# A hybrid scan, retention and attention step: modulation tiles multiplied in four visits instead of seven

## Chip, cores, metric

One core of a Trainium2 chip runs the whole program. The metric is the device time of one execution in microseconds (us), lower is better.

## The reference

Two streams share the weights of two layers: 128 context tokens and 256 latent tokens, 1024 wide. The reference runs them one after the other; the kernel runs both at once, T = 384 columns. Per layer:

```python
sh1, sc1, g1, sh2, sc2, g2 = _modulation(cond, w_ada, b_ada)   # silu(cond) @ w_ada + b_ada, 1024 x 6144
h = _rmsnorm(x, norm1_w) * (1 + sc1) + sh1
u = h @ w_in                                                    # columns for three groups of heads
y_ssd, ssd_state = _ssd(...)        # state-space scan, 8 heads of 64, two directions
y_ret, ret_state = _retention(...)  # retention with fixed decay, 4 heads of 64, two directions
y_mla, ckv, krope = _mla(...)       # latent attention, 4 heads, keys and values from a rank of 128
x = x + g1 * (concat(y_ssd, y_ret, y_mla) @ w_out)
h2 = _rmsnorm(x, norm2_w) * (1 + sc2) + sh2
x = x + g2 * (swiglu(h2 @ ffn_w1) @ ffn_w2)
```

The change concerns when one part of `_modulation` is multiplied: the 2048 columns of w_ada that give sh2 and sc2. They are needed only after attention.

## The kernel before, in words

The program is written by hand, engine by engine: each engine's instructions stand in one fixed order, and semaphores tie the engines together. The order of the calls in TensorE's block is therefore the order on the engine, and a wait holds up all that is behind it. PE is TensorE, DVE VectorE, ACT ScalarE, POOL GpSimd, and SP the engine that issues nearly all loads.

Activations lie channels on partitions, tokens along the row. Wide products run as three passes over rounded high and low halves (L475 to L477, in `split_mm`); ACT makes the high halves of weights (L1015) and DVE the low halves (L1353). All other products, those of this change too, are plain f32, and each shows in the trace as two records.

*Modulation.* `ada_block(p, k, w)` (L498) multiplies rows of w_ada. With w = 2, as in this stretch, one call handles a pair of tiles of 512 KB: for each of two halves it waits for the landing of its tile in one of four buffers of `adas` (L502), issues four products of 32 output columns by 256, one per group of 32 columns of the array, into bank 4 of PSUM (L504), and tells SP by `ada_used` that the buffer is free. The sums accumulate in bank 4 over all eight pairs, k = 0 to 7, so only the last pair ends them. In the profile one pair is 16 records of L504. SP's `load_ada` (L388 to L393) waits until the tile four places earlier is used up and then issues the load. The first four tiles of the part are loaded long ahead. When the last pair is through, DVE copies the sums (L1363, `ada_rows`), TensorE transposes them (L512, `ada_turn`) and DVE adds the bias (L1371).

*The stretch between scan and attention*, on TensorE, in order: end states of retention (L763), queries 0 and 1 (L802), the last states, **pairs 0 and 1**, retention scores of chunk 0 (L773), the rotation of the keys (L816), queries 2 and 3, **pair 2**, the sum of squares of the gated scan output (L823, waits for ACT's squares and for DVE's keys `kr`, L1728), **pair 3**, the rotation of the queries (L829), `ret_values(0)` (L785), `ret_scores(1)`, **pair 4**, `ret_values(1)` (L785 and L790), `ret_scores(2)`, **pair 5**, `ret_values(2)`, the keys of attention (L845), **pair 6**, the means of the retention output (L849), the values of attention (L858), **pair 7**, the variances (L865), then attention with the first half of the output projection between its heads (L877, seen as L475 to L477).

*Beside it.* DVE multiplies each chunk's scores by the decay matrix (L1704, `ret_probs`), which `ret_values` of the chunk waits for (L779); between these it rotates two heads' queries (L1742 to L1744). It takes the square root's inverse of L823's sums (L1381 to L1385, with ACT's L1027 and L1029 ahead). It copies the retention output to `ry` (L1746) when `ret_values(2)` is through, and L849 waits for that copy (L847). After ACT's squares of the centred output (L1264) come ACT's high halves of the mix (L1056) and, behind `ada_rows` on DVE, their low halves (L1405). The first product of the output projection waits for four of these (L926).

Of the kernel before, what the change touches and what calls it, by code (L numbers as in the profile page):

```python
# [102 lines left out]
def program(nc, x_d, const_d, small_d, win_d, wdt_d, wout_d, wf1_d, wf2_d, wada0_d, wada_d, y_d, sssd_d, sret_d, ckv_d, kr_d):  # L103
    with ExitStack() as ctx:
# [364 lines left out]
        def _(pe):  # L469
# [28 lines left out]
            def ada_block(p, k, w=1):  # L498

                for half in range(w):  # L500
                    b = k * w + half
                    pe.wait_ge(ada_in[b % 4], p * 32 + 16 * (b // 4) - 48)  # L502
                    for j in range(4):
                        last = mm(ps[j * CW:(j + 1) * CW, 4, half * 256:half * 256 + 256], cond[:, k, :],  # L504
                                  adas[:, b % 4, j * 256:(j + 1) * 256], start=(b == 0), stop=(b == w * KD - 1))
                    last.then_inc(ada_used, 1)
# [114 lines left out]
            for L in range(DEPTH):  # L621
# [145 lines left out]
                def ret_scores(c):  # L767

                    if c:
                        pe.wait_ge(rprob_ready, L * 3 + c)  # L770
                    for r in range(HR):
                        rows = slice((r % 2) * 64, (r % 2) * 64 + 64)
                        last = mm(ps[:, 2 + r % 2, (r // 2) * P:(r // 2) * P + P], u[rows, U_RK + r // 2, c * P:c * P + P],  # L773
                                  u[rows, U_RQ + r // 2, c * P:c * P + P], start=True, stop=True)
                    last.then_inc(rscore_ps, 1)

                def ret_values(c):

                    pe.wait_ge(rprob_ready, L * 3 + c + 1)  # L779
                    if c:  # L780
                        pe.wait_ge(qr_ready, L * 8 + 4 * c)
                    for m in range(2):
                        outs = [(2 * m + o, ps[o * 64:o * 64 + 64, m, c * P:c * P + P]) for o in range(2)]
                        for r, out in outs:
                            last = mm(out, kvt[:, c, 256 + r * 64:320 + r * 64], rp[:, r % 2, r // 2, :], start=True,  # L785
                                      stop=(c == 0))
                        if c:

                            for r, out in outs:
                                last = mm(out, enter_r[c - 1][:, r * 64:r * 64 + 64], qr[c - 1][:, r // 2, r % 2, :], start=False, stop=True)  # L790
                    last.then_inc(ry_ps, 1)
# [4 lines left out]
                def query(h):  # L796

                    if h >= 2:
                        pe.wait_ge(q_taken, L * HM + h - 1)
                    for k in range(2):  # L800
                        c0 = C_UQ + k * 384 + h * 96
                        last = mm(ps[0:96, h % 2, 0:T], small[:, c0:c0 + 96], u[:, U_MQ + k, :],  # L802
                                  start=(k == 0), stop=(k == 1))
                    last.then_inc(q_ps, 1)
# [12 lines left out]
                query(2)  # L817
                query(3)
                ada_block(L * 6 + 3, 2, 2)
                pe.wait_ge(gsq_ready, L * 4 + 3)  # L820
                pe.wait_ge(kr_ready, L * 3 + 3)
                for m in range(4):
                    last = mm(ps[:, 7, 0:T], ones, sq_c[:, m, :], start=(m == 0), stop=(m == 3))  # L823
                last.then_inc(ms_ready, 1)
                ada_block(L * 6 + 3, 3, 2)
                pe.wait_ge(ret_state, L * 4 + 4)
                pe.wait_ge(q_taken, L * HM + HM)
                for h in range(HM):
# [4 lines left out]
                ret_values(0)  # L833
                ret_scores(1)
                ada_block(L * 6 + 3, 4, 2)
                ret_values(1)
                ret_scores(2)
                ada_block(L * 6 + 3, 5, 2)
                ret_values(2)

                pe.wait_ge(ck_ready, L * 3 + 3)
# [1 line left out]
                for hp in range(2):  # L843
                    c0 = C_UKV + hp * 128
                    mm(ps[:, 2 + hp, 0:512], small[:, c0:c0 + 128], ck[:, 0:512], start=True, stop=True).then_inc(k_ps, 1)  # L845
                ada_block(L * 6 + 3, 6, 2)
                pe.wait_ge(ry_taken, L + 1)  # L847
                for m in range(2):
                    last = mm(ps[:, m, 0:T], cc(K_BD), ry[:, m, :], start=True, stop=True)  # L849
# [3 lines left out]
                for kt in range(4):  # L853
                    if kt == 1:
                        pe.wait_ge(k_ready, L * HM + 2)
                    if kt >= 2:
                        pe.wait_ge(vm_ready, L * 4 + kt - 1)
                    mm(ps[:, 2 if kt % 2 else 7, 0:256], ck[:, kt * P:kt * P + P], wv, start=True, stop=True)\  # L858
                        .then_inc(vm_ps, 1)
                ada_block(L * 6 + 3, 7, 2)  # L860
                pe.wait_ge(q_ready, L * 2 + 2)
                pe.wait_ge(centred, L + 1)
# [1208 lines left out]
```

## Time and profile before

| | |
|---|---|
| median of 3 runs | 1052.37 us (1051.87 to 1052.9) |
| profiled execution, first to last instruction (span) | 1048.6 us |
| busy: PE, DVE, ACT, POOL | 1026.5, 632.1, 439.6, 106.0 us |
| moved by DMA | 159.56 MB, mean 152 GB/s |
| loads of `adas` by SP | 80 of 512 KB, median 5.7 us from issue to landing |
| L504 in all | 640 records, 39.9 us |

How to read it: the profile gives the profiled execution's own time as its span alone; the median of the runs lies 3.8 us above it, for what is ahead of the first instruction and behind the last. The page's busy time is the union of an engine's instructions. A matmul's start is recorded, its end is modelled, and neighbours overlap in the records; the distance between starts tells how long one holds the engine. The stretch between scan and attention lies at 164 to 192 us in layer 0 and at 669 to 698 us in layer 1. In the views, x16 counts the records of a group, and "[0.38 <-DVE kr L1728]" is idle time of the engine before it and what ended it.

### The profile page before, as it was taken

To read this page: it belongs to the slowest core of one execution; us is meant where nothing else is said; L and a number is where in the kernel's file an instruction comes from. 1 tells how busy PE (TensorE), PEld (TensorE's weight loads), DVE (VectorE), ACT (ScalarE), POOL (GpSimd) and SP (SyncE) were. 2 spreads that over 40 slices of the span, in tenths; PEclk is the share of its full clock that TensorE was granted. 3 is DMA by queue.
4 is the path that set the end of the run, shared out by engine and by line. 5 is a ranking of instruction groups with operands and counts; after the bars stand their busy time and mean duration, and the time that the engine had idled before them with its cause. 6 is when DMAs were issued, how large, how long until landed. Compare 5 with 4: busy or idle time off the path is not lost.

```text
span 1048.6 us, 16439 instructions
## 1 busy us (share of the span) xinstructions
PE 1026.5 (98%) x6552; PEld 938.2 (89%) x6552; DVE 632.1 (60%) x1134; ACT 439.6 (42%) x684; POOL 106.0 (10%) x99
## 2 busy tenths in 40 slices
PE   7899999999999999999999999999999999999995
PEld 4698995789999989999999999668999999999995
DVE  6686868868555543534448787886765555543333
ACT  3256445446333332343334655644543333233231
POOL 0004323003000000000100223400200000000100
PEclk9999999999999999999999999999999999999998
DMA  9843245214333478333364224451243333633331
GB/s 383 330 168 124 82 161 216 115 44 165 129 131 133 168 285 321 118 112 114 135 243 161 91 88 161 161 203 41 81 142 134 125 120 120 258 105 111 126 122 60
DMA packets 30678, 159.56 MB, mean 152 GB/s; under 512 B 3424, under 2 KB 4384, under 8 KB 19872
## 3 DMA queue, kind: packets, MB, share of 16 engines
q1 hardware_dynamic: 28896, 146.75, 38.4%
q10 hardware_dynamic: 1728, 12.06, 2.8%
q8 instruction: 38, 0.62, 0.2%
q14 instruction: 16, 0.13, 0.0%
HBM read 156.27 MB, written 2.52 MB: 151 GB/s over the span
## 4 chain that ended last, share of the span: by engine, by line
PE 93%; DVE 3%; ACT 1%; issue 1%; ACTq 1%; DVEq 0%
PE ps L475 26%; PE ps L477 26%; PE ps L476 26%; PE ps L504 3%; PE ps L920 2%; PE ps L900 1%; PE ps L719 1%; PE ps L746 1%; PE ps L909 1%; PE ps L571 1%; PE ps L823 1%; ACTq L1065 1%; PE ps L802 1%; PE ps L710 0%; DVE wlo L1353 0%
## 5 line engine op out<-in xcount | busy, mean ns | idle before, releaser
L475 PE MATMUL ps<-h_hi,whi 128*128 128x386 f32 (+1 forms) x1120 | 384.9, 344 | 0.2
L477 PE MATMUL ps<-h_hi,wlo 128*128 128x386 f32 (+1 forms) x1120 | 379.7, 339 | 0.0
L476 PE MATMUL ps<-h_lo,whi 128*128 128x386 f32 (+1 forms) x1120 | 378.7, 338 | 0.0
L1353 DVE TENSOR_TENSOR wlo<-stage,whi 128x2048 fp32r<-128x2048 f32 (+1 forms) x106 | 223.3, 2106 | 154.4 <-ACT whi L1015 154.4
L1015 ACT ACTIVATE whi<-stage 128x2048 fp32r<-128x2048 f32 (+1 forms) x106 | 185.9, 1754 | 229.1 <-PE ps L477 210.5
L475 PEld LDWEIGHTS ps<-h_hi,whi 128*128 128x128 f32 x1120 | 211.3, 189 | 9.7 <-issue 7.2
L476 PEld LDWEIGHTS ps<-h_lo,whi 128*128 128x128 f32 x1120 | 211.6, 189 | 0.3
L477 PEld LDWEIGHTS ps<-h_hi,wlo 128*128 128x128 f32 x1120 | 210.6, 188 | 0.0
L475 PE MATMUL ps<-hid_hi,whi 128*128 128x384 f32 x352 | 118.3, 336 | 0.0
L477 PE MATMUL ps<-hid_hi,wlo 128*128 128x384 f32 x352 | 118.3, 336 | 0.0
L476 PE MATMUL ps<-hid_lo,whi 128*128 128x384 f32 x352 | 118.3, 336 | 0.0
L1401 DVE COPY shifted<-ps 128x4 f32<-128x4 f32 x55 | 8.8, 160 | 104.8 <-PE ps L477 104.3
L477 PEld LDWEIGHTS ps<-hid_hi,wlo 128*128 128x128 f32 x352 | 66.2, 188 | 0.0
L475 PEld LDWEIGHTS ps<-hid_hi,whi 128*128 128x128 f32 x352 | 66.2, 188 | 0.0
L476 PEld LDWEIGHTS ps<-hid_lo,whi 128*128 128x128 f32 x352 | 66.2, 188 | 0.0
L1940 POOL TENSOR_TENSOR ny<-nv 128x384 f32<-128x384 f32 x2 | 2.2, 1092 | 441.6 <-ACT nv L1319 441.6
L1412 DVE SCALAR_TENSOR_TENSOR x<-ps,modl,x 128x128 f32<-128x128 f32 x96 | 35.4, 410 | 12.2 <-PE ps L477 12.2
L504 PE MATMUL ps<-adas,cond 128*32 128x256 f32 x640 | 39.9, 383 | 0.0
L1051 ACT ACTIVATE hid_hi<-nt 128x384 f32 (+1 forms) x22 | 11.6, 525 | 51.8 <-DVE nt L1829 51.8
L1051 ACT ACTIVATE hid_hi<-ny 128x384 f32 (+1 forms) x22 | 11.6, 525 | 51.7 <-DVE ny L1829 51.7
L504 PEld LDWEIGHTS ps<-adas,cond 128*32 128x32 f32 x640 | 18.1, 109 | 16.8 <-issue 6.8
L1516 DVE SCALAR_TENSOR_TENSOR v<-upad,small,v 128x388 f32<-128x388 f32 x48 | 27.7, 620 | 4.5 <-ACT v L1127 3.9
(295 smaller groups left out, 1146.4 us busy)
## 6 DMA issues: line engine op xcount, KB each, us to landing
stage<-wf_dram SPq DMA_DIRECT2D x44, 1024.0 KB, 4.8
adas<-wada_dram SPq DMA_DIRECT2D x80, 512.0 KB, 5.7
stage<-wf_dram SPq DMA_DIRECT2D x32, 704.0 KB, 4.1
stage<-win_dram SPq DMA_DIRECT2D x20, 1024.0 KB, 4.8
stage<-wout_dram SPq DMA_DIRECT2D x8, 1024.0 KB, 5.8
adaf<-wada_dram ACTq DMA_DIRECT2D x6, 1024.0 KB, 15.0
small<-small_dram SPq DMA_DIRECT2D x2, 1202.5 KB, 8.5
stage<-win_dram ACTq DMA_DIRECT2D x2, 1024.0 KB, 13.2
```

Of the source, the lines that this page charges most:

```text
L475: mm(out, ah, bh, start=(k == 0), stop=False)
L476: mm(out, ah, bl, start=False, stop=False)
L477: return mm(out, al, bh, start=False, stop=(k == n - 1))
L504: last = mm(ps[j * CW:(j + 1) * CW, 4, half * 256:half * 256 + 256], cond[:, k, :], adas[:, b % 4, j * 256:(j + 1) * 256], start=(b == 0), ...
L571: last = mm(ps[j * CW:(j + 1) * CW, 4, half], cond[:, k, :], ada0[m][:, k, :], start=(k < 4), stop=(k >= 4))
L719: last = mm(ps[:, 5 + d, hh * P:hh * P + P], sel[:, h:h + 1].to_broadcast([P, P]), cumt[:, i0:i0 + P], start=True, stop=True)
L920: last = mm(ps[o:o + 64, 5 + h // 2, c * P:c * P + P], vm[:, k0 // P + kt, h * 64:h * 64 + 64], pt[:, a % 2, kt * P:kt * P + P], start=(kt ...
L1015: f(whi[:, g % 2, 0:width], stage[:, g % 2, 0:width], ACT.Copy).then_inc(w_hi, 1)
L1051: f(hid_hi[:, bass.ds(i * 2 + j, 1), :], (ny, nt)[j][:, 1:2, :], ACT.Copy).then_inc(hid_hi_ready, 1)
L1353: tt(wlo[:, g % 2, 0:width], stage[:, g % 2, 0:width], whi[:, g % 2, 0:width].bitcast(F32), ALU.subtract)\
L1412: last = stt(xm, ps[:, bank:bank + 1, t0:t1], gm, xm, ALU.mult, ALU.add)
L1516: ins = stt(v[:, a, :], upad[:, a, w:w + CONVT], sc(C_CW + w * 6 + a), v[:, a, :], ALU.mult, ALU.add)
```

## The change

Three calls of `ada_block` stand elsewhere in TensorE's block, for both layers. Pair 3 comes right behind pair 2, pair 5 right behind pair 4, and pair 6 right ahead of pair 7. Nothing else is changed: the same products into the same bank, the same loads in the same order.

```diff
@@ -817,12 +817,12 @@
                 query(2)
                 query(3)
                 ada_block(L * 6 + 3, 2, 2)
+                ada_block(L * 6 + 3, 3, 2)
                 pe.wait_ge(gsq_ready, L * 4 + 3)
                 pe.wait_ge(kr_ready, L * 3 + 3)
                 for m in range(4):
                     last = mm(ps[:, 7, 0:T], ones, sq_c[:, m, :], start=(m == 0), stop=(m == 3))
                 last.then_inc(ms_ready, 1)
-                ada_block(L * 6 + 3, 3, 2)
                 pe.wait_ge(ret_state, L * 4 + 4)
                 pe.wait_ge(q_taken, L * HM + HM)
                 for h in range(HM):
@@ -833,9 +833,9 @@
                 ret_values(0)
                 ret_scores(1)
                 ada_block(L * 6 + 3, 4, 2)
+                ada_block(L * 6 + 3, 5, 2)
                 ret_values(1)
                 ret_scores(2)
-                ada_block(L * 6 + 3, 5, 2)
                 ret_values(2)
 
                 pe.wait_ge(ck_ready, L * 3 + 3)
@@ -843,7 +843,6 @@
                 for hp in range(2):
                     c0 = C_UKV + hp * 128
                     mm(ps[:, 2 + hp, 0:512], small[:, c0:c0 + 128], ck[:, 0:512], start=True, stop=True).then_inc(k_ps, 1)
-                ada_block(L * 6 + 3, 6, 2)
                 pe.wait_ge(ry_taken, L + 1)
                 for m in range(2):
                     last = mm(ps[:, m, 0:T], cc(K_BD), ry[:, m, :], start=True, stop=True)
@@ -857,6 +856,7 @@
                         pe.wait_ge(vm_ready, L * 4 + kt - 1)
                     mm(ps[:, 2 if kt % 2 else 7, 0:256], ck[:, kt * P:kt * P + P], wv, start=True, stop=True)\
                         .then_inc(vm_ps, 1)
+                ada_block(L * 6 + 3, 6, 2)
                 ada_block(L * 6 + 3, 7, 2)
                 pe.wait_ge(q_ready, L * 2 + 2)
                 pe.wait_ge(centred, L + 1)
```

## Rows read from the trace of the kernel before

**Rows 1.** The page, busy time of TensorE (us, share of the span, instructions)

```profile
PE 1026.5 (98%) x6552; PEld 938.2 (89%) x6552; DVE 632.1 (60%) x1134; ACT 439.6 (42%) x684; POOL 106.0 (10%) x99
```

**Rows 2.** What TensorE waited for, 193 to 664 us: total us, times, longest us

```profile
PE ps L475 <- DVE mix_b L1405: 0.4, 1, 0.4
```

**Rows 3.** Timeline of TensorE, layer 0: start us, us, instruction [idle before <-releaser]

```profile
169.67 1.07 PE L504 MATMUL ps<-adas,cond 128*32 128x256 f32 x16
170.67 2.85 PE L823 MATMUL ps<-sq_c,const 128*128 128x384 f32 x8
...
174.45 1.97 PE L829 MATMUL ps<-qh,const 96*96 96x256 f32 x8
...
176.94 0.71 PE L773 MATMUL ps<-u 64*128 64x128 f32 x8
177.58 1.07 PE L504 MATMUL ps<-adas,cond 128*32 128x256 f32 x16
178.58 0.44 PE L785 MATMUL ps<-ew,xt 128*64 128x128 f32 x4
...
179.61 0.71 PE L773 MATMUL ps<-u 64*128 64x128 f32 x8
...
181.26 0.44 PE L785 MATMUL ps<-ew,xt 128*64 128x128 f32 x4
...
185.20 1.56 PE L849 MATMUL ps<-xt,const 128*128 128x384 f32 x4
```

**Rows 4.** Timeline of VectorE (DVE), layer 0

```profile
177.76 0.69 DVE L1704 TENSOR_TENSOR ew<-ps,upad 128x512 f32<-128x512 f32 x1 [1.13 <-PE ps L773]
...
180.52 0.69 DVE L1704 TENSOR_TENSOR ew<-ps,upad 128x512 f32<-128x512 f32 x1
...
183.27 0.96 DVE L1746 COPY xt<-ps 128x768 f32<-128x768 f32 x1
```

**Rows 5.** The chain that ended last, layer 0: start us, us, what

```profile
164.05 1.86 PE ps L504 x32
...
189.93 0.48 DVE adac L1363
...
190.54 1.97 DVE h_lo L1405 x4
...
192.55 0.45 PE ps L475
```

**Rows 6.** Loads of tiles 6 and 7, layer 0: issues, and us to landing

```profile
L393 SPq DMA_DIRECT2D adas<-wada_dram x2: 414/426/438, 165.5 to 166.0; - x2
...
DMA to landing us min/median/max: 5.4/5.8/6.2
```

**Rows 7.** Loads of tiles 6 and 7, layer 1: issues, and us to landing

```profile
L393 SPq DMA_DIRECT2D adas<-wada_dram x2: 430/430/430, 671.1 to 671.5; - x2
...
DMA to landing us min/median/max: 6.0/6.4/6.8
```

**Rows 8.** Timeline of TensorE, layer 1

```profile
674.94 1.07 PE L504 MATMUL ps<-adas,cond 128*32 128x256 f32 x16
676.39 2.82 PE L823 MATMUL ps<-sq_c,const 128*128 128x384 f32 x8 [0.38 <-DVE kr L1728]
...
680.14 1.97 PE L829 MATMUL ps<-qh,const 96*96 96x256 f32 x8
```

**Rows 9.** Timeline of all engines, layer 1, where a modulation tile landed late

```profile
690.29 0.18 PEld L504 LDWEIGHTS ps<-adas,cond 128*32 128x32 f32 x8 [0.25 <-DMA adas<-wada_dram]
...
690.88 1.56 PE L849 MATMUL ps<-xt,const 128*128 128x384 f32 x4
```

**Rows 10.** Timeline of TensorE near the kernel's start

```profile
3.65 7.21 PE L552 MATMUL ps<-upad 128*128 128x384 f32 x16 [3.65 <-DVE upad L1433]
...
36.08 0.61 PE L582 MATMUL ps<-const,adac 128*128 128x2 f32 x4 [1.22 <-DVE adac L1452]
36.54 0.34 PE L475 MATMUL ps<-h_hi,dthi 128*16 128x384 f32 x1
```

## The prediction

> **What bounds the kernel now.** I read the page first. It has TensorE busy for 98% of the span [rows 1]. Busy time of a pipelined engine says little, so next I read what TensorE waited for. From the start of attention in layer 0 to late in layer 1's scan, nearly 470 us, its longest wait was 0.4 us, for DVE's low half of the mix just behind attention, and none was for a DMA [rows 2]. Work that TensorE does itself is the bound, and whatever makes it arrive late at attention stays in the time: nothing behind waits long enough to give it back.
>
> Then the stretch of the change. The timeline of TensorE in layer 0 shows the modulation products (L504) as groups of 16 records, one group a pair of tiles [rows 3]. Beside it I read DVE's timeline [rows 4], the chain that ends the stretch [rows 5] and the landings of the modulation tiles [rows 6, 7], and for layer 1 the few rows where it differs [rows 8, 9]. What to see: TensorE goes straight from each group to the next, while the tiles that it multiplies land only shortly before it comes to them, and two of DVE's operations end just when a group of L504 does.
>
> **The edits, costed.** No instruction is added or removed. In each of two layers pair 3 moves ahead of the sum of squares (L823), pair 5 ahead of ret_values(1), and pair 6 back to pair 7.
>
> *What a visit costs.* A lone pair holds TensorE for 170.67 - 169.67 = 1.00 us [rows 3]. Pairs 0 and 1, which stand together already, hold it 1.86 us [rows 5]. So a pair put beside another costs 0.86 us, and each of three visits saved gives 0.14 us: 6 x 0.14 = 0.84 us over both layers, if nothing else happens. The tiling page of the Trainium skill (TensorEngine Tiling (Array Packing), Key Properties) states that a change of tiling mode drains TensorE. The 0.14 us agree with it, and by that rule alone the change would be a gain. It is a rival below, worked out from rows.
>
> *Pair 3 ahead of L823.* The modulation tiles have four buffers. Tiles 4 to 7 (pairs 2 and 3) can be requested only as pairs 0 and 1 are used up. In layer 0 the last two of these are issued at 165.5 and 166.0 and land 5.4 and 6.2 us later, at 170.9 and 172.2 [rows 6]. Before, pair 3 starts one lone visit ahead of L829, at 174.45 - 1.00 = 173.45, and never sees this. After, pair 2 starts at 169.67 and is through at 170.53, so pair 3 waits for tile 6 and then for tile 7. What follows the landing of a second tile is seen once: the wait for a tile ends at 690.29 and the next group starts at 690.88, so 0.59 us, and I add 0.04 us for the release [rows 9]. L823 then starts at 172.2 + 0.63 = 172.83 instead of 170.67. It holds TensorE 173.45 - 170.67 = 2.78 us, and L829 starts at 175.61 instead of 174.45: **+1.16 us in layer 0**.
> In layer 1 tile 7 is issued at 671.5 and takes 6.8 us: 678.3 [rows 7]. L823 at 678.93 instead of 676.39 (where it waited 0.38 us for DVE's kr, a wait that is now covered), L829 at 681.71 instead of 680.14 [rows 8]: **+1.57 us in layer 1**.
> The rest of TensorE's queue stands behind that wait, L823 and the root that DVE takes from it included. The root ends some 2.2 us later in layer 0 and must be done when DVE turns to the second decay product (L1704, ret_probs(1)); DVE sat idle 1.13 us before that one and it comes 1.16 us later itself [rows 4], so this just fits, with nothing added. The bounds: at 0.5 us less or more in each landing the two terms are 0.66 to 1.66 and 1.07 to 2.07; their floor, with all tiles there in time, is the rival below.
>
> *Pair 5 ahead of ret_values(1).* DVE needs the scores of chunk 2 to make what ret_values(2) reads. Before, pair 5 ran meanwhile: scores at 179.61, DVE's product from 180.52 to 181.21, values at 181.26, just as pair 5 was through [rows 3, 4]. After, counted without the shift from above: both pairs from 177.58, ret_values(1) at 179.44, scores after 179.61 - 178.58 = 1.03 us at 180.47. DVE's product began 177.76 - 176.94 = 0.82 us after the scores of chunk 1, where DVE was free. Here it is at 181.29 and ends 0.69 us later at 181.98. With 0.05 us for the release, ret_values(2) starts at 182.03 instead of 181.26, **+0.77 us**: TensorE multiplies as much as before, but the wait for DVE has lost its cover, which was pair 5.
>
> *Pair 6 moved back.* Its place before L849 gives 1.00 us, but L849 needs DVE's copy of ry (L1746). That copy starts 183.27 - 180.52 = 2.75 us after DVE's product and takes 0.96 us [rows 4], all of it DVE work in a row: 181.29 + 3.71 + 0.05 = 185.05. L849 started at 185.20 [rows 3], so it stands at -0.15 us where +0.77 would be without the move. Then pairs 6 and 7 in one visit hold TensorE 0.86 us longer than pair 7 alone. DVE's copy of the sums (L1363) waits for their end, and the chain of the stretch goes on through it: L1363, then four low halves (L1405), then TensorE's first output product [rows 5]. None of these has slack, so attention starts at -0.15 + 0.86 = **+0.71 us** against the shift from above. The ry chain bounds this from below: with no wait for DVE at all it would be -0.28 us (two visits saved), and if L849 came a full 0.77 us late it would be +1.63 us. I take 0.71 since each step has its own row. Layer 1 has the same order and nearly the same spacings, so the same 0.71.
>
> *Queues and other engines.* SP issues the same 16 loads in the same order, each as soon as the tile four before it is used up. Tile 11 is asked for at about 172.7, when tile 7 is done, and needed at 180.0 (pairs 4 and 5 start at 177.58 + 1.16 = 178.74, their last tile is 1.29 us on): 7.3 us, in layer 1 the same, where the slowest landing of rows 6 and 7 took 6.8. Tile 15 is asked for by 180.6 and needed after 190. Neither is waited for. The stores and output weights behind them on SP follow tile 15's issue, which is no later than before. ACT's work here waits on TensorE and moves with it; POOL has none of it.
>
> **Sum.** 1.16 + 1.57 + 2 x 0.71 = 4.15 us. The profiled execution spans 1048.6 us, so its span becomes 1052.8. The median of the runs, 1052.37, has 3.8 us around that span, which don't change: **1056.5 us**, +0.39%.
>
> **The rivals.**
> *The tiles land in time.* If the loads landed some 2 us earlier than in this profile, L829 would come 0.14 us earlier in layer 0. In layer 1 L823 would start at 674.94 + 1.86 = 676.80 and L829 at 679.58, 0.56 us earlier [rows 8]. The sum is then -0.14 - 0.56 + 1.42 = +0.7 us: 1053.1. For it: landings vary from load to load. Against it: both layers show the same queue of four, with the last at 6.2 and 6.8 us.
> *Only the hand-overs count* (the other side, not slower). If the waits that I see had slack that the profile hides, three hand-overs a layer fall away: 1052.37 - 0.84 = 1051.5 us. It decides this way only if tile 7 is there within 1.29 us of pair 2's start, and if DVE's product is no later than 181.3. The rows say 2.5 us and 182.0. The drain rule above is this case.
> *The clock falls.* TensorE would wait 0.4 and 0.9 us in layer 0 and 1.3 and 0.8 us in layer 1. The TensorE page of the Trainium skill (TensorE: Matmul & The Clock Gate, Loop structure matters more than you think) warns that waits for DMAs between matmuls let the clock drop. Rows bear against it here: an idle time of 1.22 us at 36.08 was followed by a wide product in 0.34 us [rows 10], what such a product takes all through the kernel. A price from rows: 16 records of the size of L823's took 7.21 us at the kernel's start [rows 10] where 2 x 2.78 = 5.56 us is the pace later, so 1.65 us a layer: 1059.8.
> *Less than all arrives.* If DVE's chain at the end hides part of pair 7's shift, or the root's wait gives some back, 0.4 us a layer goes: 1055.7, within the forecast's own range.
>
> **How the numbers follow.** 0.2% is 2.1 us, about what a measurement of this kernel can tell from no change. Forecast (with the last case), 80%: its own range is 1055.0 to 1057.8, from half a microsecond in each landing and 0.4 us a layer at the end. Tiles in time 10%, hand-overs alone 5%, clock 3%, and 2% for what I don't see. All but a little of the forecast and the clock case lie above 1054.5: slower 0.82. The next two cases are within 0.2%, and faster needs more than all hand-overs together: same 0.16, faster 0.02. The range, 1053.0 to 1058.2, takes in the tiles in time.
>
> **What would show it.** Right: L504 of pair 3 has idle time before it that a DMA on adas ends, about 1 us in layer 0 and 2 us in layer 1. L823 starts 3.1 to 3.2 us after pair 2 does in layer 0 and 4.0 us in layer 1. TensorE waits for DVE's L1704 before ret_values(2), about 0.8 us, where it did not. L849 follows L845 with a short wait for ry. Pairs 6 and 7 are one group of 32 records in 1.86 us. The distance in the chain from L504's first visit to the first output product grows from 28.50 us (164.05 to 192.55) to 30.4, and everything behind keeps its spacing. Wrong: no wait on adas, or L1704 not on the chain, or a stretch behind attention that gets shorter.

## The result, and the profile after

The change made the kernel slower, and by more than I had forecast. The median is 1059.99 us (1057.35 to 1060.83, 4 runs) against 1052.39 us; the ratio is 1.0058, 95% interval 1.0041 to 1.0076. A second set of executions gave 1058.72 us against 1052.52 us, ratio 1.0058 (1.0045 to 1.0071). My forecast was 1056.5 us, 0.39% slower, with a range that ended at 1058.2.

The profiled execution took 1059.6 us. From its first to its last instruction it spans 1057.7 us, 9.1 us more than the one before. From its page, the busy times, and the group of modulation products (busy us, mean ns, then idle time ahead of them and what ended it):

```profile
PE 1030.1 (97%) x6552; PEld 939.9 (89%) x6552; DVE 632.4 (60%) x1134; ACT 439.5 (42%) x684; POOL 106.0 (10%) x99
...
L504 PE MATMUL ps<-adas,cond 128*32 128x256 f32 x640 | 39.8, 383 | 4.4 <-DMA adas<-wada_dram 4.4
```

TensorE's busy time rose by 3.6 us [rows 1] although it has the same 6552 matmuls: some of them were slower. And L504, whose matmuls had 0.0 us of idle time ahead of them, now waits 4.4 us for a DMA. The view of TensorE's waits from 160 to 1000 us (total, times, longest) has three lines of 0.8 us or more that were not there, the first, second and fourth here. The third, the wait for `mix_b`, is as it was. The kernel before had there 0.6 us for ACT's `xt` and 0.4 us for `kr`, and both are gone:

```profile
PE ps L504 <- DMA adas<-wada_dram: 4.4, 5, 1.6
PE ps L785 <- DVE ew L1704: 1.6, 2, 0.8
PE ps L475 <- DVE mix_b L1405: 0.8, 2, 0.4
PE ps L475 <- DVE h_lo L1405: 0.8, 2, 0.4
```

L504's wait is for the tiles. L785's is the wait for DVE's product with its cover gone, 0.8 us a layer. The wait for `h_lo`, 0.4 us a layer, stands right ahead of the first output product. The timeline of TensorE in layer 0, to set beside [rows 3]. L824 is the sum of squares (L823 before) and L848 the former L849:

```profile
165.69 1.93 PE L504 MATMUL ps<-adas,cond 128*32 128x256 f32 x32
...
171.38 1.07 PE L504 MATMUL ps<-adas,cond 128*32 128x256 f32 x16
173.32 0.64 PE L504 MATMUL ps<-adas,cond 128*32 128x256 f32 x8 [0.87 <-DMA adas<-wada_dram]
174.60 0.64 PE L504 MATMUL ps<-adas,cond 128*32 128x256 f32 x8 [0.64 <-DMA adas<-wada_dram]
175.17 2.85 PE L824 MATMUL ps<-sq_c,const 128*128 128x384 f32 x8
177.85 1.89 PE L829 MATMUL ps<-qh,const 96*96 96x256 f32 x8
...
180.91 1.93 PE L504 MATMUL ps<-adas,cond 128*32 128x256 f32 x32
...
183.80 0.71 PE L773 MATMUL ps<-u 64*128 64x128 f32 x8
185.31 0.44 PE L785 MATMUL ps<-ew,xt 128*64 128x128 f32 x4 [0.79 <-DVE ew L1704]
...
188.33 1.56 PE L848 MATMUL ps<-xt,const 128*128 128x384 f32 x4
...
191.85 1.93 PE L504 MATMUL ps<-adas,cond 128*32 128x256 f32 x32
...
196.54 0.44 PE L475 MATMUL ps<-h_hi,whi 128*128 128x384 f32 x1 [0.38 <-DVE h_lo L1405]
```

Pair 2 starts 5.69 us behind pair 0, as before. Then pair 3 waits for tile 6 and for tile 7, and L829 stands at 177.85 - 165.69 = 12.16 us behind pair 0, where it was at 10.47. From L829 to the first output product the stretch takes 18.69 us where it took 18.10. Layer 1, beside [rows 8]:

```profile
673.23 1.93 PE L504 MATMUL ps<-adas,cond 128*32 128x256 f32 x32
...
678.93 0.64 PE L504 MATMUL ps<-adas,cond 128*32 128x256 f32 x8
681.21 0.64 PE L504 MATMUL ps<-adas,cond 128*32 128x256 f32 x8 [1.65 <-DMA adas<-wada_dram]
682.50 0.64 PE L504 MATMUL ps<-adas,cond 128*32 128x256 f32 x8 [0.65 <-DMA adas<-wada_dram]
683.79 0.74 PE L504 MATMUL ps<-adas,cond 128*32 128x256 f32 x8 [0.65 <-DMA adas<-wada_dram]
684.46 4.39 PE L824 MATMUL ps<-sq_c,const 128*128 128x384 f32 x8
688.69 1.89 PE L829 MATMUL ps<-qh,const 96*96 96x256 f32 x8
...
707.38 0.44 PE L475 MATMUL ps<-h_hi,whi 128*128 128x384 f32 x1 [0.38 <-DVE h_lo L1405]
```

Here three tiles are waited for, tile 5 first, and L824 takes 4.39 us where it took 2.82. The table by stretch says why. Its columns are the stretch and its length, then the busy us of PE, PEld (TensorE's weight loads), DVE, ACT and POOL, and behind them the granted clock (PEclk), the DMA share and GB/s:

```profile
18.00:22.00 4.00, 4.00 (x22) 1.55 (x23) 2.29 (x6) 0.00 (x0) 0.00 (x0) 0.57 1.01 428
...
680.00:684.00 4.00, 1.49 (x20) 0.47 (x24) 3.40 (x3) 2.35 (x3) 0.70 (x1) 1.00 0.97 359
684.00:688.00 4.00, 4.00 (x14) 2.03 (x7) 0.67 (x1) 0.00 (x0) 0.00 (x0) 0.57 0.81 268
688.00:692.00 4.00, 4.00 (x34) 2.60 (x36) 2.15 (x5) 1.10 (x2) 0.00 (x0) 1.00 0.22 91
```

In 680 to 684 us TensorE is busy for 1.49 us of 4. In the next 4 us its granted clock is 0.57 on average: the record holds a piece of 3.4 us at 0.5, which is 1.2 GHz in place of 2.4. Behind 688 it is 1.00 again. The first line is another such piece, at the start of the kernel, where nothing was changed. It costs 165.69 - 163.98 = 1.7 us in this execution. Over all thirteen profiles of this document, seven have it and start pair 0 of layer 0 at 165.5 to 165.8 us; six do not and start it at 163.9 to 164.1. Two of the three profiles of the changed kernel are among the seven, neither of the two of the kernel before is. Yet the variants of the change are on both sides, and TensorE was busy for 2.30 us of the 4 us ahead of that place in this profile and in the first one of the kernel before alike. What decides it is not known.

So the 9.1 us of the two spans are: 1.7 us at the start, 2.28 us in layer 0 (30.85 from pair 0 to the first output product, where it was 28.57), 5.17 us in layer 1 (34.15 against 28.98). Nothing came or went behind the first output product.

### The profile page after: what moved, and what is told of

It is laid out like the page before. It is cut to its first block, busy times and chain, and to the rows that moved or that the text cites. A ratio compares the mean times of both kernels' runs of the same rounds, so it can differ in the third digit from the quotient of the medians.

```text
span 1057.7 us, 16439 instructions
## 1 busy us (share of the span) xinstructions
PE 1030.1 (97%) x6552; PEld 939.9 (89%) x6552; DVE 632.4 (60%) x1134; ACT 439.5 (42%) x684; POOL 106.0 (10%) x99
## 4 chain that ended last, share of the span: by engine, by line
PE 94%; DVE 2%; DMA 1%; ACT 1%; ACTq 1%; issue 0%; POOL 0%; DVEq 0%; SPq 0%; POOLq 0%
PE ps L475 26%; PE ps L477 26%; PE ps L476 26%; PE ps L504 3%; PE ps L920 1%; DMA adas<-wada_dram 1%; PE ps L900 1%; PE ps L824 1%; PE ps L571 1%; PE ps L719 1%; PE ps L746 1%; PE ps L909 1%; ACTq L1065 1%; PE ps L802 1%; PE ps L710 0%; PE ps L552 0%
## 5 line engine op out<-in xcount | busy, mean ns | idle before, releaser
L475 PE MATMUL ps<-h_hi,whi 128*128 128x386 f32 (+1 forms) x1120 | 384.9, 344 | 0.8 <-DVE h_lo L1405 0.8
L475 PEld LDWEIGHTS ps<-h_hi,whi 128*128 128x128 f32 x1120 | 211.3, 189 | 10.4 <-issue 7.2
L475 PE MATMUL ps<-hid_hi,whi 128*128 128x384 f32 x352 | 118.3, 336 | 0.0
L475 PEld LDWEIGHTS ps<-hid_hi,whi 128*128 128x128 f32 x352 | 66.2, 188 | 0.0
L504 PE MATMUL ps<-adas,cond 128*32 128x256 f32 x640 | 39.8, 383 | 4.4 <-DMA adas<-wada_dram 4.4
L504 PEld LDWEIGHTS ps<-adas,cond 128*32 128x32 f32 x640 | 18.2, 109 | 20.9 <-DMA adas<-wada_dram 6.9
L1931 POOL TENSOR_TENSOR sq<-sq 128x384 f32<-128x384 f32 x12 | 15.7, 1310 | 147.9 <-ACT sq L1032 147.3
```

What stands on the lines that cost most here:

```text
L475: mm(out, ah, bh, start=(k == 0), stop=False)
L1931: g.tensor_tensor(sq[:, 0, :], sq[:, 0, :], sq[:, k, :], ALU.add).then_inc(sq_summed, 1)
```

## The experiments

My theory after this profile: pair 3 now waits for tiles that were requested too late, the landings vary from execution to execution, and behind the longest waits the clock falls. Pairs 5 to 7 cost what I had said. The rivals were that the loss sits in the order on TensorE and DVE, or in something else of the program.

### One move at a time

**Pair 3 alone.**

```diff
                 ada_block(L * 6 + 3, 2, 2)
+                ada_block(L * 6 + 3, 3, 2)
...
                 last.then_inc(ms_ready, 1)
-                ada_block(L * 6 + 3, 3, 2)
```

> Only pair 3 is moved, ahead of L823; pairs 5 and 6 stay in their old places. Theory A, TensorE waits for tiles 5 to 7 and its clock then falls once in layer 1: this part carries nearly all of the loss, since after the whole change L829 stood 1.7 us later in layer 0 and 4.6 us in layer 1 (the kernel's start taken out), so 1052.4 + 6.3 = 1058.7 us, idle time before L504 that a DMA on adas ends of about 4 us in all, and a granted clock of 0.5 for some 3 us behind it in layer 1. Rival B, the wait as I forecast it and no clock: 1052.4 + 2.7 = 1055.1 us. Rival C, the loss comes from something else in the changed program (its start, or a moved pair 5 or 6): within 1 us of 1052.4.

Measured: 1055.72 us median (1054.94 to 1059.98) against 1052.32 us, ratio 1.0035 (1.0022 to 1.0049). Six of the eight executions lie between 1054.9 and 1055.8 us, two at 1058.3 and 1060.0. The profile is of one of these two: L504 waits 4.0 us for DMAs, L829 stands 3.7 and 3.5 us later than before, and the clock fell in both layers. The median is nearest to rival B, the profiled execution to theory A. (The mean granted clock of the other high one, 0.991, is the lowest of the eight.) This move alone brings the waits and the fallen clock, but its size is no fixed number.

**Pair 5 alone.**

```diff
                 ada_block(L * 6 + 3, 4, 2)
+                ada_block(L * 6 + 3, 5, 2)
                 ret_values(1)
                 ret_scores(2)
-                ada_block(L * 6 + 3, 5, 2)
                 ret_values(2)
```

> Only pair 5 is moved, ahead of ret_values(1). My step says 0.77 us a layer, because DVE's product of chunk 2 (L1704) has lost its cover: 1053.9 us, an idle time of about 0.8 us before ret_values(2) in each layer, no wait on adas, clock unchanged. Rival, only the hand-over counts: 1052.4 - 0.3 = 1052.1 us and no idle time before L785.

Measured: 1056.06 us (1054.67 to 1057.92), ratio 1.0036 (1.0022 to 1.005). That is more than twice what I expected. The timeline of TensorE in its layer 0 shows both causes:

```profile
179.23 1.50 PE L504 MATMUL ps<-adas,cond 128*32 128x256 f32 x24
182.19 0.64 PE L504 MATMUL ps<-adas,cond 128*32 128x256 f32 x8 [1.45 <-DMA adas<-wada_dram]
...
185.29 0.44 PE L785 MATMUL ps<-ew,xt 128*64 128x128 f32 x4 [0.79 <-DVE ew L1704]
```

The last row is the wait for DVE's L1704, 0.79 us, as expected. The second is a wait of 1.45 us for tile 11, which I had excluded. Tile 11 can be requested only when tile 7 is used up. Counted from pair 0, it was requested here at 10.6 us, needed at 15.1 and landed at 16.5. In layer 0 of the whole change it was requested at 9.6, one us sooner, landed at 14.5, and was needed only at 16.5, because the waits of pair 3 had put pair 5 off. So no wait of pair 5 is seen there. A step that is free in one order is not free in another.

**Pair 6 alone.**

```diff
-                ada_block(L * 6 + 3, 6, 2)
                 pe.wait_ge(ry_taken, L + 1)
...
+                ada_block(L * 6 + 3, 6, 2)
                 ada_block(L * 6 + 3, 7, 2)
```

> Only pair 6 is moved, to pair 7. By my steps L849 comes 0.92 us earlier (at 184.28, when DVE's copy of ry is done), and pairs 6 and 7 then hold TensorE 0.86 us longer ahead of DVE's copy of the sums: -0.06 us a layer, 1052.3 us. Rival, the moved pair delays the chain through L1363 by its full 0.86 us since L849 waits for ry anyway: 1054.1 us.

Measured: 1051.96 us (1051.19 to 1054.17), ratio 0.9999 (0.999 to 1.0009). In the profile the stretch is 0.06 us shorter in layer 0 and 0.17 us longer in layer 1. The move alone costs and gives nothing; the rival's 0.86 us a layer, 1.7 us in all, lies above the interval, which ends at 0.9 us.

### The loads taken out

**The change without the loads of tiles 6 and 7.** SP signals the tile as landed once its buffer is free, and pair 3 multiplies the old contents.

```diff
                     sp.wait_ge(ada_used, p * KD + b + 1)
+                    if w == 2 and b in (6, 7):
+                        sp.sem_inc(ada_in[b % 4], 16)
+                        continue
                     sp.dma_start(adas[:, b % 4, :], ...
```

> The change, but tiles 6 and 7 of the moved part are not loaded: SP signals them as soon as their buffer is free, and pair 3 multiplies what lies there (sh2 and sc2 are wrong by that pair). Theory A, the landing of tiles 6 and 7 and the clock behind it are the loss: L829 comes as early as in the kernel before or earlier (-0.14 and -0.56 us), what is left is 0.6 us a layer from pairs 5 to 7: 1052.9 us, and the clock doesn't fall at this place. Rival B, the loss lies in the order on TensorE and DVE, not in the loads: still 1056 us or more.

Measured: 1052.48 us against the change's 1058.72 and 1052.52 before; ratio to before 1.0004 (0.9994 to 1.0015). All of the loss that can be measured goes with the landings of two tiles. TensorE's waits in its profile (lines are 3 further down, so L788 is L785 and L478 is L475):

```profile
PE ps L788 <- DVE ew L1707: 1.6, 2, 0.8
PE ps L478 <- DVE mix_b L1408: 0.8, 2, 0.4
PE ps L478 <- DVE h_lo L1408: 0.8, 2, 0.4
```

No line of L504 is left, the clock doesn't fall in the stretch, L829 stands 10.24 and 10.25 us behind pair 0, and the wait for DVE, 1.6 us in two, is still there. One trace of a tile remains in layer 0: the group of pairs 4 and 5 holds TensorE some 0.2 us longer than the 1.93 us in the change, and the weight loads in it waited for the DMA, by the landings tile 11.

```profile
179.00 2.16 PE L507 MATMUL ps<-adas,cond 128*32 128x256 f32 x32
```

With pair 3 early and not held up, tile 11 just misses its time there.

**With pair 5 put back** in addition:

```diff
-                ada_block(L * 6 + 3, 5, 2)
                 ret_values(1)
                 ret_scores(2)
+                ada_block(L * 6 + 3, 5, 2)
                 ret_values(2)
```

> As the last one, but pair 5 is back between ret_scores(2) and ret_values(2). My step on pair 5 (the wait for DVE's L1704 loses its cover) says that this takes the rest away: no idle time before ret_values(2), hand-overs saved and nothing lost, 1052.4 - 0.7 - 0.1 = 1051.6 us, 1.3 us less than with pair 5 moved. Rival, the wait before ret_values(2) is hidden behind DVE's ry chain anyway: equal to the kernel with pair 5 moved within 0.4 us.

Measured: 1051.64 us (1049.48 to 1054.97), ratio 0.9991 (0.9977 to 1.0005). The waits:

```profile
PE ps L478 <- DVE mix_b L1408: 0.8, 2, 0.4
PE ps L478 <- DVE h_lo L1408: 0.8, 2, 0.4
```

L785's wait is gone too. Its profile and that of the kernel before are both without a fallen clock and can be compared directly: 1047.7 against 1048.6 us, 0.9 us less, where I expected 0.8. That is what the hand-overs and most of one wait for kr are worth with no other wait put in their place. The 0.8 us between the two medians (1.3 expected) are within their scatter; the rows show the wait.

**Tile 7 alone not loaded**, by `if w == 2 and b == 7:` in the edit above.

> The change, with tile 7 alone not loaded (pair 3's second half multiplies what lies in its buffer; sh2 and sc2 are wrong by that half). It is the half dose of the kernel without tiles 6 and 7. Tiles land some 1.27 us apart, so if the last landing sets the start of L823, L829 comes about 0.85 us earlier a layer than in the change (tile 6 at its old time, then 0.43 us of products), and the clock falls less often: 1055.5 to 1057.5 us, between 1052.5 and 1058.7. If the loads were not the cause: 1058.7 us.

Measured: 1055.95 us (1051.8 to 1057.42), with 1052.9 us before, ratio 1.0024 (1.0013 to 1.0036). That lies between the 1.0004 with neither tile loaded and the 1.0058 of the change, so taking out one load of two takes away about half of the loss. In its profile layer 1 still waits 1.9 us, for tiles 5 and 6, and the clock falls behind that.

### The clock

**Three products between pairs 2 and 3**, so that TensorE works while it waits:

```diff
                 ada_block(L * 6 + 3, 2, 2)
+                pe.wait_ge(ret_state, L * 4 + 4)
+                for _ in range(3):
+                    mm(ps[:, 6, 0:T], ident, const[:, K_U:K_U + T], start=True, stop=True)
                 ada_block(L * 6 + 3, 3, 2)
```

> The whole change, and between pair 2 and pair 3 three products of a constant by constants (1.9 us of TensorE at full clock) into an unused bank, so that TensorE works while tile 6 is awaited; their result is not used. Theory A, the clock falls because TensorE stands idle in layer 1: the clock stays up there, L823's line takes 2.7 us and not 4.2, and the median is 1.5 us or more below that of the change, 1058.5 us or less. Rival B, the whole loss is in the waits for tiles and for DVE: the same 1060.0 us as the change, or up to 0.5 us more for the added products.

> The change with three products of constants between pairs 2 and 3, again, this time beside the changed kernel itself. The clock theory: 1.5 to 3 us below it although TensorE has 3.8 us more to do, no granted clock under 1 in the stretch. Without the clock: no faster than the changed kernel.

Measured: 1057.14 us (1056.11 to 1058.77), and beside the changed kernel 1057.82 us (1056.16 to 1061.06) against its 1058.72. The first was measured in another set than the change. In the second set the ratios to before, 1.0053 (1.0039 to 1.0067) with the products and 1.0058 (1.0045 to 1.0071) without, overlap, so the times don't show a gain. The medians there differ by 0.9 us, not by the 1.5 us that I expected: the added products don't fit wholly into the wait, and in three of the four layers profiled L829 stands some 0.6 us later than tile 7's landing asks for. The rows do show the clock staying up. In both profiles, four layers, no piece at 0.5 lies in the stretch, though tile 7 landed as late as in the change, 9.6 to 10.3 us behind pair 0. From the second one, the same columns as above:

```profile
176.00:180.00 4.00, 4.00 (x16) 2.44 (x15) 0.56 (x2) 1.10 (x2) 0.00 (x0) 1.00 0.78 292
...
684.00:688.00 4.00, 4.00 (x26) 1.95 (x25) 1.61 (x1) 0.00 (x0) 0.00 (x0) 1.00 0.83 286
```

### More profiles of both kernels

The second set gave another profile of the change. Two single executions, one of each kernel, were profiled besides.

> The changed kernel itself, to have it on the same chip and in the same rounds as the next three, with a second profile of it. Theory (waits for tiles 5 to 7 that vary from run to run, and a clock that falls behind some of them): a median of 1058 to 1061 us, runs up to 3 us apart, and in the profile some 2 to 4 us of idle time before L504 that a DMA ends. Rival, the first four runs were a freak of one chip: near 1056.5 us, my forecast.

> The kernel before, for a second profile: where tile 7 lands, counted from the start of pair 0. Chance alone sets it: anywhere from 8.2 to 10.5 us, as over all profiles so far. The moved pair 3 delays the landing: 8.2 to 9.3 us, as in the six layers in which pair 3 is in its old place, against 8.9 to 10.5 where it is moved.

> The changed kernel, for a third profile on the same chip: tile 7 lands 8.9 to 10.5 us behind the start of pair 0 in both layers, L829 starts 12.2 us or more behind it, and where the wait for tiles is over, the granted clock is 0.5 for 3.4 us in most layers.

This execution of the changed kernel took 1054.19 us, far below the nine others, of which the lowest took 1057.35. What I expected of it after the first two profiles, late landings and a fallen clock in most layers, did not come. It is the execution that I had forecast before any. Layer 0 and layer 1, timelines of TensorE:

```profile
169.67 1.07 PE L504 MATMUL ps<-adas,cond 128*32 128x256 f32 x16
170.99 0.64 PE L504 MATMUL ps<-adas,cond 128*32 128x256 f32 x8 [0.25 <-DMA adas<-wada_dram]
172.27 0.64 PE L504 MATMUL ps<-adas,cond 128*32 128x256 f32 x8 [0.64 <-DMA adas<-wada_dram]
172.84 2.85 PE L824 MATMUL ps<-sq_c,const 128*128 128x384 f32 x8
175.52 1.89 PE L829 MATMUL ps<-qh,const 96*96 96x256 f32 x8
```

```profile
670.81 1.93 PE L504 MATMUL ps<-adas,cond 128*32 128x256 f32 x32
...
679.95 0.64 PE L504 MATMUL ps<-adas,cond 128*32 128x256 f32 x8 [0.66 <-DMA adas<-wada_dram]
680.52 2.85 PE L824 MATMUL ps<-sq_c,const 128*128 128x384 f32 x8
683.21 1.89 PE L829 MATMUL ps<-qh,const 96*96 96x256 f32 x8
```

Its tiles land as in [rows 6, 7]. L829 is at 175.52, and I had said 175.61. In layer 1 it is 683.21 - 670.81 = 12.40 us behind pair 0, 1.51 us later than before, and I had said 1.57. The clock did not fall. The span is 1052.1, and I had said 1052.8.

The second profile of the kernel before had late landings. Tile 5 landed 7.2 and 7.7 us behind the start of pair 0 (5.7 and 6.0 in the first profile), and its layer 1 reads

```profile
678.01 0.64 PE L504 MATMUL ps<-adas,cond 128*32 128x256 f32 x8 [1.41 <-DMA adas<-wada_dram]
678.58 2.85 PE L823 MATMUL ps<-sq_c,const 128*128 128x384 f32 x8
```

so the unchanged kernel waits too, 2.3 us in its two layers, but for tile 5 only. It took 1052.57 us, the median of its kernel, and its span is 2.2 us longer than that of the first profile. Tile 7 landed at 9.7 and 10.3 us, which refutes the rival as I had put it, 8.2 to 9.3 us with pair 3 in its old place. Over all profiles with these loads tile 7 lands at 8.2 to 10.3 us (mean 9.2, 8 layers) with pair 3 in its old place and at 8.3 to 10.5 (mean 9.6, 12 layers) where it is moved. Its load is requested 2.0 to 2.6 us behind pair 0 in every one of them, before pair 2 has even begun, so the moved pair of the same layer can't hold it up. Whether the half microsecond between the means is more than scatter, these few layers don't show.

In the second profile of the change the clock fell in layer 0 already:

```profile
173.94 0.64 PE L504 MATMUL ps<-adas,cond 128*32 128x256 f32 x8 [1.53 <-DMA adas<-wada_dram]
175.21 0.64 PE L504 MATMUL ps<-adas,cond 128*32 128x256 f32 x8 [0.63 <-DMA adas<-wada_dram]
175.78 4.50 PE L824 MATMUL ps<-sq_c,const 128*128 128x384 f32 x8
180.12 1.89 PE L829 MATMUL ps<-qh,const 96*96 96x256 f32 x8
```

L824 takes 4.50 us, 1.65 us more than the 2.85 at full clock. From the start of pair 3's second half to L829 it is 4.91 us, where it is 3.25 in layer 0 of the first profile of the change. In its layer 1 the fall came earlier, from 684.3 to 687.7 us, and took in the two halves of pair 3:

```profile
685.50 1.08 PE L504 MATMUL ps<-adas,cond 128*32 128x256 f32 x8 [0.21 <-DMA adas<-wada_dram]
686.51 3.44 PE L824 MATMUL ps<-sq_c,const 128*128 128x384 f32 x8
689.78 1.89 PE L829 MATMUL ps<-qh,const 96*96 96x256 f32 x8
```

The same distance is 4.28 us here. Part of the slow piece lay in time that was waited away in any case, and the fall cost 1.0 us.

## Why the prediction was right or wrong

- **The bound, and that nothing behind gives it back.** Right. From the first output product of layer 0 to pair 0 of layer 1 the distance is the same, 476.7 us, before and after.
- **The clock rival at 3%, and at nothing in the sum.** This is the step that failed most. The profiles with pair 3 moved, all tiles loaded and nothing filled in have eight layers. The clock fell in five of them, and also in layer 1 without tile 7. Four of these six falls cost 1.6 to 1.65 us each, as priced, and two cost 0.9 and 1.0 us. I held against it one wait of 1.22 us behind which the pace was full [rows 10], though my own forecast had two waits in a row in layer 1, 1.3 and 0.8 us. Pair 3 waits for two or three tiles in a row, with half a visit's work between the waits. Ahead of the six falls these waits had come to 2.95 us (1.65, 0.65 and 0.65), 2.2, 1.9, 1.9, 1.8 and 1.8 us. In the four other layers with such waits they came to 1.6, 1.5, 0.9 and 0.3 us, and the clock stayed up. These are the layers seen, no rule: the fall at the kernel's start had no such difference ahead of it. With products in the wait, and no more than a single wait of 1.4 us left, the clock did not fall in four layers. That speaks for idle TensorE, and not the late tile itself, as what the clock answers to.
- **That the rival's 1059.8 us is near the measured 1059.99 and 1058.72 is partly luck.** It stands for a fall in both layers at the landings of the first profile. The profiled execution of the change had one fall in the stretch and one at the start.
- **Pair 3 waits for tile 7.** The mechanism was right, and so was its size for the landings that I had: L829 was forecast at 175.61 and seen at 175.52. The landing itself was mis-sized. I took 172.2 and 678.3 from one execution and gave each half a microsecond. Counted from pair 0, tile 7 was at 8.2 and 9.1 us there; in the change's first two profiles it was at 8.9 and 10.5, 9.5 and 10.0. The profile of before happened to be one of the quick ones. A hint stood in it: the two layers already differed by 0.9 us. In the difference of the two kernels, though, much of this cancels, because a late tile 5 holds up the kernel before as well. An estimate from rows: in the change L829 starts 3.30 us behind the landing of tile 7. With the landings of the second profile of the kernel before (9.74 and 10.27 us) it would start at 13.04 and 13.57, where it started at 11.58 and 12.09 there. That is 1.5 us later in each layer, where 1.16 and 1.57 were forecast.
- **The sum for the profiled execution of the change.** Its span is 4.9 us above the forecast 1052.8. The later landings of tile 7 give 0.7 and 1.4 us, the fall in layer 1 1.65 and the fall at the start 1.7, less some 0.5 us by which smaller terms came out lower.
- **A visit costs 0.14 us.** Right in its sign, and in its total partly by luck. With the waits for tiles out of the way, the change less pair 5 takes 192.33 - 164.05 = 28.28 us in layer 0 from pair 0 to the first output product, against 28.57: 0.29 us for two visits fewer. But 0.22 of it is gained up to L829, by pair 3's visit alone, where 0.14 was forecast, and 0.07 behind, where pair 6's gain is held by DVE's copy of ry. (In layer 1 it is 0.53 us, because most of L823's wait of 0.38 us for kr [rows 8] goes too.) What the Trainium skill states, that a change of tiling mode drains TensorE (TensorEngine Tiling (Array Packing), Key Properties), agrees with a gain of that kind. It was the smallest term.
- **Pair 5, +0.77 us; pairs 6 and 7, +0.71 in all.** Right in the mechanism. L829 to the first output product grew by 0.59 us in each layer, 0.12 less than forecast. L785's wait is 0.79 us, and L849 lands on DVE's copy of ry as said. But my reason why tile 11 would not be waited for did not hold for each order of the moves; pair 5 alone showed the other case.
- **The root for DVE's second product just fits.** Right: in layer 0 the root ends at 181.12 us and L1704 starts at 181.15, and nothing waits for it.
- **3.8 us around the span.** Wrong. The runs list span and time together: 1.8 us lie around it (1050.8 and 1052.57 in the second profile of the kernel before), and 1.7 to 2.1 around the three profiled executions of the change. So the first profile was of an execution some 2 us quicker than the median, about what tile 5's waits took in the second. The forecast of a median from one quick profile inherited that.

What stays open: pair 3 alone cost 3.4 us in the median and the whole change 6.2 and 7.6 in its two sets, while pairs 5 to 7 add 1.2 us in the rows (0.59 + 0.59). The rest may be the share of executions in which the clock falls, in the stretch or at the start, which may differ between sets of four to eight executions; it was not settled. The three single moves' losses add up to 6.8 us (3.4 + 3.7 - 0.4), but that is no account of the change: pair 5 alone has a wait for tile 11 that the change has not. Nor is it known why tile 5 lands late in some executions. It landed more than 7 us behind pair 0 in two of the ten layers 0 and in six of the ten layers 1 that have all loads, and never in the four layers in which tiles 6 and 7 were not loaded behind it (5.5 to 6.2 us). That these loads slow it is a rival that no run here decides.

## What to carry to other kernels

A visit to a stream of tiles doesn't only cost its own hand-over; it paces the stream. With four buffers and 3 to 8 us from request to landing, as tiles 4 to 7 had here, the gaps between visits are what the loads hide in, and putting visits together turns them into waits. Before moving a consumer, write down for each tile when its buffer is freed and when it is needed, add the slowest landing of several executions and not the one at hand, and do this again for each combination of moves. Put the same landings into the kernel before, since what is late may hold up both. If the waits that come out stand on TensorE one behind the other, give the price of a clock at half rate a large chance, and not 3%.

## What the runs showed of the hardware that was not expected

The granted clock fell to 0.5 for 3.4 us behind several short waits with half-pair products between them. A fall cost 1.6 to 1.65 us where all of it lay in the products behind the waits (L824 took 4.26 to 4.50 us in place of 2.85), and 0.9 to 1.0 us where part of it lay in the waits. The same can happen near the start of the kernel, 17.9 to 19.4 us in, in some executions and not in others, at 1.7 us. And one load of 512 KB, tile 5's, issued 1.1 us behind pair 0 each time, landed 5.3 to 7.9 us behind pair 0 in the profiles, of both kernels. Where it landed later than 7 us, those queued behind it followed at 1.3 us each, so its lateness was handed to all.
